# Grid attention: the excess tiles of a pair transposed whole into one PSUM bank instead of in halves into two

## What is computed

```python
s_loc = einsum('bqhd,bkhd->bhqk', qr, ks) * scale + bias   # masked to the window's columns
s_ctx = einsum('bqhd,bchd->bhqc', qr, kc) * scale
p = softmax(concat([s_loc, s_ctx], -1))
out = einsum('bhqk,bkhd->bqhd', p[..., :n_loc], vs) + einsum('bhqc,bchd->bqhd', p[..., n_loc:], vc)
```

## Time and profile before

| | |
|---|---|
| median of three runs | 2589.29 us (2588.93 to 2590.97) |
| the profiled execution, its time | 2585.25 us |
| its span in the profile | 2583.2 us |
| PE busy | 2524.3 us, 98% |
| DVE, ACT, POOL busy | 59%, 31%, 9% |
| granted clock of TensorE | 0.997 of full speed |
| grid attention in the span | about 1501 to 1600 us |

### The profile page before, as it was taken

The page is one execution under the profiler, slowest core; times in us unless marked ns, Lnnn a source line. Parts: engine busy times, 40 slices in busy tenths (PEclk is TensorE's granted clock), DMA queues, the critical chain, the costliest instruction groups (busy, mean ns, idle before and its releaser), DMA issues.

```text
span 2583.2 us, 37879 instructions
## 1 busy us (share of the span) xinstructions
PE 2524.3 (98%) x14263; PEld 1854.8 (72%) x14263; DVE 1521.1 (59%) x3851; ACT 795.9 (31%) x1753; POOL 242.3 (9%) x426
## 2 busy tenths in 40 slices
PE   6999999999999999999999999999999999999999
PEld 3477688777778686566688776868578776546867
DVE  2357677599866664443443477757868574415554
ACT  2236511177731123332210066112312364121211
POOL 1100100000011000000043023310000002011000
PEclk9999999999999999999999999999999999999999
DMA  7021000021112221310001112533231104225321
GB/s 270 24 103 46 26 33 33 33 74 46 42 54 91 81 85 63 101 39 28 26 22 43 33 49 43 111 106 102 109 115 33 70 22 129 91 83 227 111 105 53
DMA packets 73861, 190.93 MB, mean 74 GB/s; under 512 B 7261, under 2 KB 10017, under 8 KB 72753
## 3 DMA queue, kind: packets, MB, share of 16 engines
q0 software_dynamic: 27456, 96.97, 11.7%
q1 hardware_dynamic: 45472, 91.16, 10.1%
q10 hardware_dynamic: 752, 0.38, 0.0%
HBM read 145.79 MB, written 43.04 MB: 73 GB/s over the span
## 4 chain that ended last, share of the span: by engine, by line
PE 93%; DVE 3%; ACT 1%; issue 1%; DMA 0%; ACTq 0%; DVEq 0%
PE psum L1522 36%; PE psum L1884 11%; PE psum L1824 8%; PE psum L1908 6%; PE psum L1927 5%; PE psum L1924 5%; PE psum L2012 4%; PE psum L1745 3%; PE psum L1636 3%; PE psum L1508 1%; PE psum L1489 1%; PE psum L2084 1%; PE psum L2102 1%; PE psum L2071 1%; PE psum L1901 1%
## 5 line engine op out<-in xcount | busy, mean ns | idle before, releaser
L3485 ACT ACTIVATE RP<-RP,small 128x1280 f32<-128x1280 f32 (+11 forms) x274 | 252.7, 923 | 180.8 <-DVE small L2996 180.7
L1884 PE MATMUL psum<-RQ 64*128 64x256 f32 (+5 forms) x1344 | 293.8, 493 | 2.3 <-DVE small L2996 1.5
L2996 DVE CUSTOM_DVE_ANT_0 RP<-psum,small 128x512 f32<-128x512 f32 (+1 forms) x382 | 201.6, 573 | 108.8 <-PE psum L1908 86.5
L1824 PE MATMUL psum<-RW,hT 128*128 128x512 f32 (+3 forms) x640 | 231.0, 516 | 1.0 <-ACT hT L3215 1.0
L1884 PEld LDWEIGHTS psum<-RQ 64*128 64x128 f32 (+1 forms) x1344 | 145.9, 187 | 83.8 <-issue 52.6
L1824 PEld LDWEIGHTS psum<-RW,hT 128*128 128x128 f32 x640 | 134.6, 215 | 82.2 <-issue 64.6
L1522 PE MATMUL psum<-RW,hT 128*128 128x256 f32 x800 | 181.5, 379 | 0.0
L3505 ACT ACTIVATE RP<-psum 128x512 f32<-128x512 f32 (+1 forms) x248 | 128.2, 530 | 134.1 <-PE psum L1908 124.1
L1522 PEld LDWEIGHTS psum<-RW,hT 128*128 128x128 f32 x800 | 151.8, 190 | 23.2 <-issue 2.1
L1927 PE MATMUL psum<-RQ,RP 128*128 128x128 f32 x1312 | 159.8, 276 | 0.5 <-ACT YR L3519 0.5
L1908 PE MATMUL psum<-ident,RP 128*128 128x128 f32 x1084 | 151.3, 279 | 7.9 <-DVE RP L3018 3.6
(11 more groups left out here) (512 smaller groups left out, 4069.8 us busy)
## 6 DMA issues: line engine op xcount, KB each, us to landing
RW<-in_w_in SPq DMA_DIRECT2D x7, 2048.0 KB, 8.1
RW<-in_od_w_ada SPq DMA_DIRECT2D x6, 2048.0 KB, 8.6
RW<-in_ev_w_in SPq DMA_DIRECT2D x5, 2048.0 KB, 7.8
RW<-in_od_w_in SPq DMA_DIRECT2D x5, 2048.0 KB, 7.9
RQ<-in_ev_w_ada SPq DMA_DIRECT2D x4, 2048.0 KB, 19.3
RX<-in_x POOLq DMA_DIRECT2D x12, 512.0 KB, 7.6
y_even<-YR POOLq DMA_DIRECT2D x20, 256.0 KB, 2.3
RP<-y_even POOLq DMA_DIRECT2D x20, 256.0 KB, 3.5
```

Source lines behind the costliest of these rows:

```text
L1824: last = pe.matmul(main.bank(f)[:, c0:c0 + nc_], lhs_of(st["lhs"], j["t"], kk), w, start=kk == 0, stop=kk == kn - 1)
L1884: last = pe.matmul(main.bank(f)[:, 0:pc["w"]], q, kk[:, keys], start=i == 0, stop=i == len(u["qk"]) - 1)
L2996: drained(main, dve.tensor_tensor_reduce(pair_slot(st, u, lane)[:, pc["at"]:pc["at"] + pc["w"]], main.bank(f)[:, 0:pc["w"]], add, -scale, ...
L3485: fn(pr, pr, ACT.Exp, bias=mins[:, at, lane, n - 1:n], scale=-1.0, accum_out=total).then_inc(s_pexp, 1)
```

## The change

The excess chunk of a unit of the grid attention gets one fill of `main` in place of two. Its side is "act" for even query tiles and "dve" for odd ones (`at % 2`, where `at` counts the units). PE transposes its two tiles whole, 128 columns each, and one engine copies 256 columns. The chunk of eight tiles keeps its halves. The copies' wait on `s_chunk` and the count by which a chunk raises it stay as they are.

```diff
                 if kind in ACROSS:
                     for ch in u["turns"][:-1]:
-                        ch["halves"] = [main.new("act"), main.new("dve")]
-                        ch["f"] = ch["halves"][1]
+                        ch["f"] = main.new("dve" if at % 2 else "act")
...
                         ring = ch["ring"]
-                        if k in ACROSS:
+                        if "halves" in ch:
                             for f in ch["halves"]:
                                 ring.wait_free(pe, f)
...
                             ring = ch["ring"]
+                            if k in ACROSS and "halves" not in ch:
+                                if ring.side[ch["f"]] == "dve":
+                                    ring.wait_full(dve, ch["f"])
+                                    if ch["c"] >= 4:
+                                        dve.wait_ge(s_chunk, ch["c"] - 2)
+                                    n = len(ch["tiles"]) * P
+                                    drained(ring, dve.tensor_copy(pair_turned(ch["c"])[:, 0:n], ring.bank(ch["f"])[:, 0:n]), ch["f"])
+                                continue
...
                             ring = ch["ring"]
+                            if k in ACROSS and "halves" not in ch:
+                                if ring.side[ch["f"]] == "act":
+                                    ring.wait_full(act, ch["f"])
+                                    if ch["c"] >= 4:
+                                        act.wait_ge(s_chunk, ch["c"] - 2)
+                                    n = len(ch["tiles"]) * P
+                                    ring.consumed(fn(pair_turned(ch["c"])[:, 0:n], ring.bank(ch["f"])[:, 0:n], ACT.Copy), ch["f"])
+                                continue
```

## The result

The changed kernel takes 2594.06 us (median of 14 runs, 2591.07 to 2595.69); the kernel before, on the same chips, 2588.68 us (14 runs, 2583.87 to 2590.97). That is +5.4 us, a ratio of 1.0020 with a 95% interval of 1.0013 to 1.0028, so between 3.4 and 7.2 us. The forecast was 2593.8 us within 2590 to 2597.

What follows compares the result with a forecast made beforehand. PE's own program length was taken as the limit in the changed pairs. 24 x (0.23 + 0.09 - 0.13) = +4.6 us moved the median 2589.29 to 2593.9, rounded down to 2593.8 us, range 2590 to 2597.

Steps and rivals of the forecast that it cites:

- part 5: Score banks in the grid attention: five fills instead of six loosen a wait that PE does not show, so nothing gained.
- Parts 1 and 2: PE transposes in 24 grid pairs: four halves removed save 0.13 us, two whole ones add 0.23, together +0.10 each.
- Part 3: New seam on PE from whole to half transposes: 0.09 us in each of 24 pairs, bounds 0 and 0.19.
- Part 4: Excess copies in the grid attention: DVE 1.9 us and ACT 0.6 us fewer, but hidden, so nothing on the path.
- The sum: Grid attention stage: 24 x (0.23 + 0.09 - 0.13) = +4.6 us, with nothing behind the stage swallowing it.
- The small stalls at the borders: Borders of head pairs: scores take 1.42 us against 1.28; DVE's spare time may shorten them, so 2593.9 rounded to 2593.8.
- The signs: Interior grid pairs: transposes 0.87 us instead of 0.68, pairs 3.33 to 3.39; stage 4.6 longer, DVE 1.9 less busy.
- A: Rival at the whole-to-half passage: seam hidden, +2.4 us, 2591.7; chance 0.20 together with E.
- B: Rival at the seam: full drain of 0.19 us in each of 24 pairs, +7.0 us, 2596.3; chance 0.17.
- C: Rival in the grid attention: copying engines set the pace, DVE's 1.9 us come off, 2587.4; chance 0.06.
- D: Rival at the single excess copy: ends 0.11 us later, ACT pairs stall, +5.8 us, 2595.1; chance 0.07.
- E: Rival on PE: a whole transpose costs the same as two halves, 2589.3 or 2591.5 with seam; 0.20 together with A.

Runs made afterwards that it cites:

- e6: Changed kernel with all 24 single copies of the excess on ACT: stage 101.12 us, 2594.96 us in one run.
- e7: Changed kernel with all 24 single copies of the excess on DVE: stage 101.18 us, 2593.59 us in one run.
- e5: Changed kernel with the eight tiles also transposed whole, four to a bank: stage 113.51 us, 2601.33 us in one run.
- e4: Changed kernel with the chunks turned round on PE, DVE and ACT, halves first, whole ones last: stage 104.40 us, 2596.64 us in one run.
- e1: Kernel before with only the excess tiles transposed whole, two fills and two copies kept: stage 101.29 us, 2595.14 us against 2588.93.
- e8: Kernel before with DVE's excess bank numbered and written ahead of ACT's: stage 95.33 us, 2586.58 us against 2588.93; again 2586.01 against 2589.88.
- e9: Kernel before with ACT copying its half of the eight tiles first, the excess last: stage 107.26 us, 2601.34 us beside 2591.47.
- e10: Kernel of e8 with the ACT and DVE banks ending window and dilated attention units also turned round: 2587.23 us against 2589.88.

## Why the prediction was right, point by point

- *What bounds it.* PE's program in the changed units: right, apart from the short waits of part 5. e6 and e7 move 9 us of copies without a trace in the stage.
- *Parts 1 and 2*, 0.13 us for four halves and 0.115 for a whole tile. The halves: confirmed by 0.68 and 0.55. The price of the whole ones was a mean over ten, in which the entry into the group is spread; the two of e5 take 0.28, 0.14 each.
- *Part 3, the seam at 0.09 us*: mis-sized. Two whole ones and the passage take 0.37 us where I had 0.32, so with 0.23 for the two, the seam is 0.14. The row of the window attention was the right one and showed the leaving (0.09, as in e4 and e5); what I missed is that a group pays an entry too, 0.05, of which the price of 0.115, a mean over ten, held only a tenth. Read by groups it is 0.28 for two whole ones and 0.09 for the passage. The transposes therefore cost 0.24 us a unit, not 0.19: 5.9 us in all, not 4.6. The rule of the Trainium skill ("TensorEngine Tiling (Array Packing)", Tiling Modes, Key Properties) that a change of mode drains the array agrees with the trace: 0.17 us idle stand before the weight loads at the new passage as well (before those of the values, where the shape changes too, it is 0.33). Before the half transposes of the changed kernel:

```profile
1511.28 0.20 PEld L1907 LDWEIGHTS psum<-ident,RP 128*128 128x128 f32 x2 [0.17 <-issue]
1511.65 0.57 PEld L1900 LDWEIGHTS psum<-ident,RP 64*128 64x128 f32 x16 [0.17 <-issue]
1512.14 0.95 PEld L1883 LDWEIGHTS psum<-RQ 64*128 64x128 f32 x8
```

- *Part 4, copies at nothing*: right. The 256-column copies take 0.42 us on DVE and 0.37 on ACT, as worked out by size.
- *Part 5, "A wait is loosened that PE does not show, so nothing is gained"*: this step failed. The wait on ACT's copy was there, 1.7 us of it, and the changed kernel has none of it. I had taken the absence of a named wait for its absence. The uneven pairs, 3.14 and 3.20 us, stood in the rows that I quoted, and I gave no reason for them. In part the reason I gave was wrong too: most of the wait goes because the longer transposes shift the scores (e1), at most 0.16 us because of the bank and the single copy.
- *The sum*: 4.6 forecast, 4.1 in the stage, 5.4 by the medians (3.4 to 7.2). Two errors, 1.3 us too little loss and 1.7 us of gain not seen, nearly cancelled. The direction and most of the size come from parts 1 to 3; that the total came so close to the forecast is luck.
- *The small stalls at the borders*, which I thought DVE might shorten: 1.42, 1.37 and 1.37 us became 1.37, 1.36 and 1.37, worth 0.06. In e8 and e1, too, one border takes 1.43, so this may be chance.
- *The signs.* Units take 3.38 to 3.39 us, at the upper end of 3.33 to 3.39, and DVE is 1.8 us less busy in the stage (82.77 to 80.99), as forecast. The transposes take 0.91 to 0.92 us where I had written 0.87.
- *Rivals.* A is refuted by e4 and e5. B was half right: the transposes alone cost 5.9 us, above the line of 5.2, and without the give-back the change would have been slower by more than 0.2%. C and D are refuted by e6 and e7, E by e5.

## What to carry to other kernels

Price a small edit on a saturated TensorE by the starts of whole groups, and count how often the shape of the array changes, entry and exit, before you count columns. When equal units take unequal times, look for the reason before you call a wait hidden: a short wait can sit in every second unit though no row names it (0.05 us here, and 0.4 in e9). In a ring of banks, find which engine reads the bank that the next fill needs, and number the fills so that the earlier reader comes first. In the grid this cost no instruction and gave 1.7 us; in the window attention the same edit had the readers the wrong way round (e10), so look it up for each stage.

## What the runs showed of the hardware that was not expected

- A change of the array's shape costs TensorE 0.09 us on leaving (halves 0.55 to 0.64 us; two whole ones 0.28 to 0.37) and 0.05 us at the start of the next group (scores 1.23 to 1.28).
- A wait of 0.4 us in front of one of two matmuls that lie on different rows of the array appears as busy time of PE and as no wait (e9: scores 1.64 us, no releaser named). Of the wait the record's duration shows 0.1 us at most: 480 ns, where it is 376 without the wait.
- The same instructions ahead of the stage took 3.9 us longer in one execution, nearly all of it in the two stretches in which the clock stood longer at its lower level (granted clock 0.74 against 0.91 from 20 to 40 us, 0.91 against 1.00 from 520 to 540), while a stage of 100 us in the middle repeats to within 0.01 us (e8: 95.33 and 95.32).
